# Head norms inside the loop of a differential attention, and the projection that follows interleaved with the last heads

## The reference

```python
logits = jnp.einsum('bqhcd,bkhcd->bhcqk', q_blk, k) * scale + bias    # c: the two maps
p = jax.nn.softmax(logits, axis=-1)
w = p[:, :, 0] - lam * p[:, :, 1]
o = jnp.einsum('bhqk,bkhe->bqhe', w, v)
...
o = o * lax.rsqrt(jnp.mean(o * o, axis=-1, keepdims=True) + EPS)
y_attn = (o.astype(h.dtype) * subln_w * (1.0 - lambda_init)).reshape(bsz, seqlen, DA_WIDTH)
return jnp.concatenate([y_ssd, y_attn], axis=-1) @ w_out
```

## Time and profile before

| | us |
|---|---|
| median of three runs | 2237.02 |
| lowest, highest | 2236.89, 2237.18 |
| the profiled execution's own time | 2237.89 |
| its span in the trace | 2236.1 |

### The profile page before, as it was taken

One profiled execution on the slowest core, in us unless ns is written; L12 is line 12 of the kernel. 1 busy time (PEld: TensorE's weight loads), 2 busy tenths in 40 slices (PEclk: granted clock), 3 DMA queues, 4 the chain that ended last, 5 costly groups with the idle time before them and its releaser, 6 DMA issues.

```text
span 2236.1 us, 29473 instructions
## 1 busy us (share of the span) xinstructions
PE 2175.4 (97%) x10276; PEld 1788.4 (80%) x10276; DVE 828.0 (37%) x1496; ACT 781.1 (35%) x1210; POOL 1103.0 (49%) x1484
## 2 busy tenths in 40 slices
PE   7999999999999989999999999999999999999999
PEld 5888888878887668886888888888777887888887
DVE  4222211844832546134222222207742464013234
ACT  4232223225424434323332223325544243222233
POOL 4555555763243214833555555544544456545554
PEclk9999999999999989999999999999999999999999
DMA  5332233222122112521232233322121313332322
GB/s 204 105 102 94 97 110 103 86 95 66 48 94 80 57 40 77 162 68 60 91 102 94 94 103 97 102 94 76 65 79 64 104 57 108 99 104 94 104 85 76
DMA packets 58909, 203.46 MB, mean 91 GB/s; under 512 B 6296, under 2 KB 7704, under 8 KB 58824
## 3 DMA queue, kind: packets, MB, share of 16 engines
q1 hardware_dynamic: 53568, 192.96, 26.8%
q10 hardware_dynamic: 5256, 9.30, 1.2%
HBM read 200.12 MB, written 4.74 MB: 92 GB/s over the span
## 4 chain that ended last, share of the span: by engine, by line
PE 76%; issue 9%; POOL 8%; DVE 5%; ACT 1%; POOLq 0%; DVEq 0%; ACTq 0%
PE bank L458 21%; PE bank L460 20%; PE bank L459 20%; POOL w_lo L422 8%; PE bank L611 2%; PE bank L613 2%; PE bank L612 2%; PE bank L793 1%; PE bank L816 1%; PE bank L720 1%; PE bank L941 1%; PE bank L922 1%; DVE prob L1878 1%; PE bank L729 1%; PE bank L1005 1%
## 5 line engine op out<-in xcount | busy, mean ns | idle before, releaser
L422 POOL TENSOR_TENSOR w_lo<-w_raw,w_hi 128x256 fp32r<-128x256 f32 x1448 | 1080.6, 778 | 1104.3 <-ACT w_hi L1137 1103.4
L458 PE MATMUL bank<-gx_hi,w_hi 128*128 128x512 f32 (+1 forms) x1776 | 686.2, 386 | 21.2 <-DVE gx_lo L1610 5.6
L460 PE MATMUL bank<-gx_hi,w_lo 128*128 128x512 f32 (+1 forms) x1776 | 677.4, 381 | 0.0
L459 PE MATMUL bank<-gx_lo,w_hi 128*128 128x512 f32 (+1 forms) x1776 | 677.0, 381 | 0.0
L1137 ACT CAST w_hi<-w_raw 128x1024 fp32r<-128x1024 f32 x364 | 379.0, 1045 | 363.5 <-PE bank L460 317.1
L458 PEld LDWEIGHTS bank<-gx_hi,w_hi 128*128 128x128 f32 x1776 | 335.9, 189 | 92.8 <-issue 9.9
L460 PEld LDWEIGHTS bank<-gx_hi,w_lo 128*128 128x128 f32 x1776 | 335.8, 189 | 64.3
L459 PEld LDWEIGHTS bank<-gx_lo,w_hi 128*128 128x128 f32 x1776 | 336.2, 189 | 62.4 <-issue 0.2
L458 PE MATMUL bank<-ff_hi,w_hi 128*128 128x512 f32 x352 | 136.9, 389 | 0.0
L459 PE MATMUL bank<-ff_lo,w_hi 128*128 128x512 f32 x352 | 136.9, 389 | 0.0
L460 PE MATMUL bank<-ff_hi,w_lo 128*128 128x512 f32 x352 | 136.9, 389 | 0.0
(11 more groups left out here) (343 smaller groups left out, 2721.3 us busy)
## 6 DMA issues: line engine op xcount, KB each, us to landing
w_raw<-wstream SPq DMA_DIRECT2D x364, 512.0 KB, 3.5
bias_spread<-bias_rows ACTq DMA_DIRECT2D x1, 2560.0 KB
x<-xT ACTq DMA_DIRECT2D x2, 1024.0 KB, 10.5
outT<-ple_o SPq DMA_DIRECT2D x8, 256.0 KB, 2.0
square<-bias_spread ACTq DMA_DIRECT2D x4, 256.0 KB, 2.7
rfin_row<-bias_spread ACTq DMA_DIRECT2D x4, 256.0 KB, 2.7
m_T<-memT ACTq DMA_DIRECT2D x1, 1024.0 KB, 5.5
p_T<-pT ACTq DMA_DIRECT2D x1, 512.0 KB, 4.3
```

Of the source, the lines that this page charges most:

```text
L422: ins = nc.gpsimd.tensor_tensor(w_lo[:, s, part], w_raw[:, s, part], w_hi[:, s, part].bitcast(F32), ALU.subtract)
L458: nc.tensor.matmul(dst, hi, rhs[0], start=first, stop=False)
L459: nc.tensor.matmul(dst, hi, rhs[1], start=False, stop=False)
L460: return nc.tensor.matmul(dst, lo, rhs[0], start=False, stop=last)
```

## The change

The norm of a head moves into the loop, two iterations behind the head itself. In iteration h, PE places `head_stat(h - 2)` in the middle of the first ssd half (so that half is now two pieces of 6 matmuls) and the new `head_row(h - 2)` between the last score and the second ssd half. DVE's `variance` stands inside `combine`, before its last piece; `normed` stands ahead of the copies of the turned map and `low` behind them. ACT's `high` stands behind the exponentials. The root and the reciprocal become one operation on POOL, `pow` with an exponent of -0.5 (`head_factor`, 128x4), and POOL's list, a loop over units until now, is written out here with one `head_factor` ahead of each unit. All eight ssd units are now inside the loop, which ends at iteration 7. Beside the last head stand the chunks of the first three `mix_attn` tiles: nine matmuls a chunk, in banks 2 to 4, with the turn, the values, and the norms of heads 6 and 7 between them. Banks of `mix_attn` change accordingly (`shift`), and the row of factors now goes to bank 0 in the loop, so `values` of the next head waits for `normed`.

```diff
+        STAT_AT = 384
+        STAT_BANK = [7] * (AH - 2) + [1, 5]
+        ROW_BANK = [0] * (AH - 2) + [1, 6]
...
+            def head_factor(h):
+
+                cut = slice(h * TT, (h + 1) * TT)
+                pool.wait_ge(sem("o_mean"), h + 1)
+                nc.gpsimd.tensor_tensor(o_rstd[:, cut], o_root[:, cut], minus_half, ALU.pow)\
+                  .then_inc(sem("o_col"), 1)
+
             up, ple = (UNIT0[n] // RING for n in ("up_a", "ple2a"))
-            rounds(0, up + 1)
+            after = UNIT0["mix_ssd"] + RING + 1
+            nc.gpsimd.memset(minus_half, -0.5).then_inc(sem("minus_half"), 1)
+            rounds(0, after // RING)
+            split_unit(after // RING, 0)
+            pool.wait_ge(sem("minus_half"), 1)
+            for h in range(AH):
+                head_factor(h)
+                if h < AH - 2:
+                    split_unit((after + h) // RING, (after + h) % RING)
+            split_unit((after + AH - 2) // RING, (after + AH - 2) % RING)
+            rounds((after + AH - 2) // RING + 1, up + 1)
...
+                wait(pe, sem("o_nrmd"), h if h < AH - 1 else h - 1)
...
+                if h == AH - 2:
+                    pe.wait_ge(tile_free, TILE0["mix_attn"])
+                if h == AH - 1:
+                    pe.wait_ge(sem("wT_act"), AH)
...
-            for h in range(AH + 2):
-                if h < AH:
-                    for n in range(3):
-                        score(h, n // 2, n % 2)
-                if h < AH - 1:
-                    ssd_half(h, 0)
-                elif h == AH:
-                    ssd_half(AH - 1, 0)
-                    ssd_half(AH - 1, 1)
-                if 0 < h <= AH:
-                    turn(h - 1)
-                if h < AH:
-                    for n in range(3, 8):
-                        score(h, n // 2, n % 2)
-                    if h < AH - 1:
-                        ssd_half(h, 1)
-                if 0 < h <= AH:
-                    values(h - 1)
-                if h > 1:
-                    head_stat(h - 2)
-            pe.wait_ge(sem("o_col"), 1)
...
+            def head_row(h):
+                pe.wait_ge(sem("o_col"), h + 1)
                 for t in range(TT):
+                    mm = nc.tensor.matmul(bank[ROW_BANK[h]][:, t * P:(t + 1) * P],
                                           o_rstd[:, h * TT + t:h * TT + t + 1].to_broadcast([P, P]), ident,
                                           start=True, stop=True)
                 mm.then_inc(sem("o_row"), 1)
 
+            def attn_part(j, k):
+
+                if k == 0:
+                    pe.wait_ge(unit_lo, UNIT0["mix_attn"] + j + 1)
+                if k == 0 and j < 3:
+                    pe.wait_ge(sem("score_read"), 8 * AH)
+                if k == 0 and j > 4:
+                    pe.wait_ge(tile_free, TILE0["mix_attn"] + j - 4)
                 pe.wait_ge(sem("o_lo"), k + 1)
+                mm = products((UNIT0["mix_attn"] + j) % RING, k, bank[(j + 2) % 5][:, :], (o_hi[:, k, :], o_lo[:, k, :]),
+                              k == 0, k == DC - 1)
+                if k == DC - 1:
+                    mm.then_inc(unit_done, 1)
+
+            def attn_chunk(k):
+                for j in range(3):
+                    attn_part(j, k)
+
+            for h in range(AH):
+                for n in range(3):
+                    score(h, n // 2, n % 2)
+                ssd_part(h, range(0, 2))
+                if h > 1:
+                    head_stat(h - 2)
+                ssd_part(h, range(2, 4))
+                if h > 0:
+                    turn(h - 1)
+                for n in range(3, 8):
+                    score(h, n // 2, n % 2)
+                if h > 1:
+                    head_row(h - 2)
+                ssd_part(h, range(4, 8))
+                if h > 0:
+                    values(h - 1)
+            attn_chunk(0)
+            turn(AH - 1)
+            head_stat(AH - 2)
+            attn_chunk(1)
+            head_row(AH - 2)
+            attn_chunk(2)
+            values(AH - 1)
+            attn_chunk(3)
+            head_stat(AH - 1)
+            attn_chunk(4)
+            head_row(AH - 1)
+            for k in range(5, DC):
+                attn_chunk(k)
+            for j in range(3, 8):
+                for k in range(DC):
+                    attn_part(j, k)
...
+            def high(h):
+                act.wait_ge(sem("o_nrmd"), h + 1)
+                nc.scalar.copy(o_hi[:, h, :], o_nrm[:, h % 2, :]).then_inc(sem("o_hi"), 1)
...
+                if h == AH:
+                    act.wait_ge(unit_done, UNIT0["mix_attn"])
+                    act.dma_start(m_T[:, :, :], memT.rearrange("(m p) s -> p m s", p=P)).then_inc(sem("m_in"), 16)
+                if h > 1:
+                    high(h - 2)
                 if h > 0:
                     act.wait_ge(sem("o_copied"), h)
                     wait(act, sem("o_stat"), h - 1)
                     nc.scalar.activation(o_sq[:, :], o_un[:, h - 1, :], ACT.Square).then_inc(sem("o_squared"), 1)
-            act.wait_ge(unit_done, UNIT0["mix_attn"])
-            act.dma_start(m_T[:, :, :], memT.rearrange("(m p) s -> p m s", p=P)).then_inc(sem("m_in"), 16)
-            act.wait_ge(sem("o_mean"), 1)
-            nc.scalar.activation(o_root[:, :], o_root[:, :], ACT.Sqrt)\
-              .then_inc(sem("o_rooted"), 1)
-            for h in range(AH):
-                act.wait_ge(sem("o_nrmd"), h + 1)
-                nc.scalar.copy(o_hi[:, h, :], o_nrm[:, h % 2, :]).then_inc(sem("o_hi"), 1)
...
+            def variance(h):
+                dve.wait_ge(sem("o_stat"), h + 1)
+                nc.vector.scalar_tensor_tensor(out=o_root[:, h * TT:(h + 1) * TT],
+                                               in0=bank[STAT_BANK[h]][:, STAT_AT:STAT_AT + TT], scalar=1.0 / AV,
+                                               in1=o_eps[:, h * TT:(h + 1) * TT], op0=ALU.mult, op1=ALU.add)\
+                  .then_inc(sem("o_mean"), 1)
+
+            def normed(h):
+                dve.wait_ge(sem("o_row"), h + 1)
+                wait(dve, sem("o_lo"), h - 1)
+                nc.vector.scalar_tensor_tensor(out=o_nrm[:, h % 2, :], in0=o_un[:, h, :], scalar=subln[:, :],
+                                               in1=bank[ROW_BANK[h]][:, :], op0=ALU.mult, op1=ALU.mult)\
+                  .then_inc(sem("o_nrmd"), 1)
...
+            def low(h):
+                dve.wait_ge(sem("o_hi"), h + 1)
+                nc.vector.tensor_tensor(o_lo[:, h, :], o_nrm[:, h % 2, :], o_hi[:, h, :].bitcast(F32), ALU.subtract)\
+                  .then_inc(sem("o_lo"), 1)
...
+                    if i == TT - 1 and beside is not None:
+                        variance(beside)
...
-            dve.wait_ge(sem("o_stat"), AH)
-            nc.vector.scalar_tensor_tensor(out=o_root[:, :], in0=bank[7][:, 384:384 + TT * AH], scalar=1.0 / AV,
-                                           in1=o_eps[:, :], op0=ALU.mult, op1=ALU.add).then_inc(sem("o_mean"), 1)
-            dve.wait_ge(sem("o_rooted"), 1)
-            nc.vector.reciprocal(o_rstd[:, :], o_root[:, :]).then_inc(sem("o_col"), 1)
...
+            for h in range(AH):
+                dve.wait_ge(sem(f"bias_in{h % 2}"), 16 * (h // 2 + 1))
+                if h >= 2:
+                    dve.wait_ge(sem("turned"), h - 1)
+                for n in range(3):
+                    biased(h, n)
                 if h > 0:
+                    combine(h - 1, h - 2 if h > 1 else None)
+                for n in range(3, 8):
+                    biased(h, n)
+                if h > 1:
+                    normed(h - 2)
                 if h > 0:
+                    weights_copied(h - 1)
+                if h > 1:
+                    low(h - 2)
+                if h == AH - 1:
+                    combine(h)
                 if h > 0:
+                    values_copied(h - 1)
+                dve.wait_ge(unit_done, UNIT0["mix_ssd"] + h + 1)
+                nc.vector.tensor_tensor(x[:, h, :], bank[1][:, :], x[:, h, :], ALU.add).then_inc(tile_free, 1)
+            weights_copied(AH - 1)
+            variance(AH - 2)
+            normed(AH - 2)
+            values_copied(AH - 1)
+            low(AH - 2)
+            variance(AH - 1)
+            normed(AH - 1)
+            low(AH - 1)
```

73 lines of the change are left out of this document (21 added, 52 removed).

## The result

| | before | after |
|---|---|---|
| median of the runs, us | 2236.95 (4 runs, 2234.18 to 2237.18) | 2219.80 (4 runs, 2218.06 to 2223.06) |
| profiled execution's own time, us | 2237.89 | 2218.06 |
| its span, us | 2236.1 | 2216.3 |

The ratio of after to before is 0.9933, with an interval of 0.9921 to 0.9945: faster, by about 15 us. The two medians of the table stand 17.2 us apart; with four runs each, the text goes by the ratio and its interval. The forecast of 2225.3 us is a ratio of 0.9948. The median lies 1.7 us under my range's lower end of 2221.5; the ratio times the 2237.02 of the forecast, 2222.0, lies inside it. Later series put the gain a little lower (see the experiments).

What follows compares the result with a forecast made beforehand. TensorE, busy 97% of the span, was taken as the bound. Its list to the first `mix_attn` addition ended at 851.9 instead of 863.6 us, so 2237.0 - 11.7 = 2225.3 us, range 2221.5 to 2231.5.

Steps and rivals of the forecast that it cites:

- PE as the end of the sum: PE's list, walked from the copy of the first head's values to the first `mix_attn` addition: 11.7 us less.
- The period: An iteration, 2 to 7, takes 15.19 us instead of 13.85: 0.81 for a moved row, 0.53 new.
- The wait for bank 1: Iterations 2 to 7: PE's first ssd product waits for DVE's addition to `x`, about 0.5 to 0.6 us each.
- The end: From the copy of head 6's values to the first `mix_attn` addition: 22.8 us, each dependent step behind a chunk.
- POOL's power: The `pow` on POOL, taken as 0.7 us; hidden up to 4.8 in the loop, about 1.5 and 1.75 at the end.
- (1): Power of 1.5 to 5 us: PE waits at the rows of heads 6 and 7, such as 2228.7 us; chance 0.12.
- (2): Long power: PE stands at `head_row` every iteration, slower from 6 us; chance 0.05, and 0.02 for merely eating the gain.
- The port (3): In the loop, POOL's power holds up DVE's last map piece: 1 to 3.6 us, up to 2229; chance 0.07.
- The clock (4): TensorE falls to half clock with the loop's 0.6 us waits: 2229 us once, 2233 twice; chances 0.07 and 0.03.
- Cover at the end (5): The end's waits partly return as a weight unit, bank or `o_lo` holds a chunk up: 3.6 us, 2229; chance 0.03.
- The whole gain arrives.: Behind the first `mix_attn` tile nothing differs but the banks, so all 11.7 us arrive in the kernel's time.
- ACT's root and its table load: The root leaves ACT; `m_root` then needs the 1.28 us table load, hidden in 3.39 us of idle time.

Runs made afterwards that it cites:

- e3: The changed kernel, with DVE adding the ssd tile to `x` before the values are copied: 2218.49 us, 0.9930 of before.
- e9: The same kernel as e3, run again in a later series: 2218.45 us, 0.9930 of before.
- e5: The changed kernel, with each head's power on POOL made four times over: 2230.82 us, 0.9983 of before.
- e6: The changed kernel, with the root back on ACT and the reciprocal on DVE, head by head: 2223.05 us, 0.9946 of before.
- e4: The changed kernel without chunks beside the last head, all eight placed after its steps; norms stay in the loop: 2233.80 us, 0.9992 of before.
- e1: The kernel before the change, run again unchanged: 2234.75 us, 0.9997 of before.
- e2: The kernel after the change, run again unchanged: 2220.49 us, 0.9939 of before.
- e7: The kernel of e4 plus 24 useless matmuls between the steps of the end: 2230.05 us, 0.9976 of before.

## Why the prediction was right

- **PE as the end of the sum.** Right: the gain is in the stretch that I walked and its size is nearly what PE's list gives, 12.3 to 12.8 us against 11.7.
- **The period.** 15.22 us measured, 15.19 worked out. The wait for bank 1 came back in all six iterations at 0.62, 3.7 us in total. e3 and e9 take it away and gain 3.2 to 3.3 us in the loop. The loop was to take 91.1 and took 91.3.
- **The end.** All waits are gone and the clock stays at 1.00. From the copy of head 6's values to the first tile it was to take 22.8 and takes 22.0; this is the mis-sized term. The turn pushes the next step back by 1.09 us (828.77 to 829.86), and I had its whole duration of 1.31. For the values I had 2.35, the time to the start of their copy, but PE goes on 2.08 behind their start (835.81 to 837.89), and likewise its first chunk starts at 826.61, 0.28 ahead of the copy of head 6's values. These three make 0.22 + 0.27 + 0.28 = 0.8 us. They belong to an operation's latency and not to PE's list. One slip had no effect: the row of head 7 has two chunks between itself and chunk 7, not three; the 4.3 us are those of two.
- **POOL's power.** I took 0.7; it is 1.01 alone and 1.45 beside DVE. Also hidden, so no term changes. e5 shows the cover: 1.8 us at the end, where the power takes 1.01, and in the loop at least the 4.7 us that four powers take there (756.75 to 761.46), where one takes 1.45. So rivals (1) and (2) did not happen because the power is short. The place where (1) has PE wait exists, as e5's 4.9 us of waits show. My 0.7 was too low by 0.3 to 0.75 us. No row had bounded it, so that the error stayed inside the cover was luck.
- **The port (3).** It did not happen. DVE's piece of two SBUF operands takes 0.74 us at 754.76 with POOL waiting beside it, and POOL's power is the one that gets longer, 1.45 instead of 1.01. The Trainium skill (SBUF — State Buffer, two separate sides) has the one that starts first keep the shared port; here DVE's piece followed the variance directly and kept it, and the trace agrees: in e6, where POOL is idle there, the piece takes the same 0.74. Since the stretch is as long in e6, the pair costs PE nothing.
- **The clock (4).** It stayed at 1.00 in the loop with a wait of 0.62 in each iteration, in the three profiles of after.
- **Cover at the end (5).** PE waits for nothing at the end; e4 shows what it covers: 4.5 us of waits and as much again of slow clock.
- **"The whole gain arrives."** Right in kind: the three ratios of after give 12 to 15 us for a stretch of 12.3 to 12.8. But "behind the first tile nothing differs" is only true of the program. Its time differs by up to 2.7 us at one place between two executions of one kernel, and whole spans by 5.6 us (before, e1) and 6.6 us (after, e2). I had walked one execution as the base. It was slow at all four places (2237.89), and the 2237.02 of the forecast stands 2 to 3 us above the medians of before in the later series. The median of after, 2219.80, lies 5.5 us under the forecast, below my range. At most 1.1 of these are the stretch's, whose gain I had as 11.7; the rest lies in stretches that differ from execution to execution.
- **ACT's root and its table load.** Costed at nothing, and the load ran in idle time ahead of `m_root` as forecast. e6 shows that two loads an iteration are hidden too.

## What to carry to other kernels

Look for the stretches in which the bounding engine waits more than once in a row, and price them as wait plus slow clock: here the clock was as much as the waits (e4: 4.8 and 4.5 us). Independent products of the next stage between the dependent steps take away both; even products that compute nothing take away the second, for the price of their own time. Before a difference of two profiles is explained, cut both at the same instructions and see which stretches also vary within one kernel: here that is 7.5 of 19.8 us.

## What the runs showed of the hardware

- A power on GpSimd with four columns takes 1.01 us (1.09 from start to start), more than a subtraction of 256 columns (0.70). How the price grows with the columns was not run.
- Behind a wait of 2.6 us TensorE fell to a lower clock in some executions and not in others of the same kernel, with the same wait: 39.1 or 41.8 us for one stretch. A fall costs 1.4 to 3.1 us at the places seen. What decides between them stays open.
- At the start of the launch products of 512 columns took 0.63 us until 20.3 or 24.4 us and 0.40 after that, while PEclk read 1.00 (after, before).
- With 24 useless matmuls in its waits a kernel's end took 28.43 us instead of 31.34, and its time was some 3.6 us lower (e4, e7; one profile each, and the intervals just touch).
